# Reordering the stages ahead of the experts of a decoder-layer step

## The reference, cut to what matters

```python
h = x + W_o( sigmoid(g_a) * Mamba2_SSD(n) + sigmoid(g_b) * ShortConv(n) ),  n = RMSNorm(x)
h = h + CrossAttn(RMSNorm(h), mem)    # 4 heads over 256 memory tokens
h = h + MoE(RMSNorm(h))               # top-4 of 32 experts, clamped SwiGLU, softmax router
y = RMSNorm(h)

def rmsnorm(x, g):
    y = xf * lax.rsqrt(jnp.mean(xf * xf, axis=-1, keepdims=True) + EPS)
    return (y * g.astype(jnp.float32)).astype(x.dtype)

# samples, one step of the recurrence (per head h, p: 64 rows, n: 128 columns)
s = jnp.exp(dtt * a)[:, :, None, None] * s + jnp.einsum('bh,bhp,bhn->bhpn', dtt, xt, bt)
y = jnp.einsum('bhpn,bhn->bhp', s, ct)

# short convolution and merge
u, new_sbuf = causal_dwconv(sconv_buf, sc_c * sc_v, lw['w_sconv'], None)
merged = jax.nn.sigmoid(g_a) * y_a + jax.nn.sigmoid(g_b) * (sc_b * u)
```

## Time and profile before

| what | value |
| --- | --- |
| median of 3 runs | 1551.15 us (1549.5 to 1552.83) |
| profiled execution: own time / span in the trace | 1553.77 / 1551.6 us |
| PE busy | 1462.9 us, 94% |
| DVE / ACT / POOL busy | 449.6 / 216.3 / 26.1 us |
| mean granted TensorE clock | 0.968 |
| HBM traffic | 490.31 MB, mean 316 GB/s |

### The profile page before, as it was taken

How to read it: one execution, slowest core, us unless ns; L and a number is a source line. 1 busy time by engine, 2 the same in 40 slices (tenths; PEclk the granted TensorE clock), 3 DMA queues, 4 the chain that set the end, 5 groups by cost and what they waited for, 6 DMA issues and landing times.

```text
span 1551.6 us, 16659 instructions
## 1 busy us (share of the span) xinstructions
PE 1462.9 (94%) x6505; PEld 745.5 (48%) x6505; DVE 449.6 (29%) x891; ACT 216.3 (14%) x392; POOL 26.1 (2%) x42
## 2 busy tenths in 40 slices
PE   7999999988598799999999999999999999999997
PEld 5888888665377583333333333333333333333332
DVE  2630030486613423222222222212213213213213
ACT  2111311311112221101101101001001001001002
POOL 0000000012000000000000000000000000000000
PEclk8999999989699888999999999999999999999999
DMA  5634443337124683999999999999999999999993
GB/s 156 248 131 145 162 161 121 115 118 248 68 109 152 253 356 120 399 430 429 427 429 427 429 429 428 428 428 428 429 429 427 429 428 428 430 427 429 429 428 152
DMA packets 68776, 490.31 MB, mean 316 GB/s; under 512 B 8483, under 2 KB 9915, under 8 KB 44157
## 3 DMA queue, kind: packets, MB, share of 16 engines
q1 hardware_dynamic: 65372, 478.61, 75.0%
q0 software_dynamic: 3184, 11.31, 2.2%
q10 hardware_dynamic: 196, 0.07, 0.0%
HBM read 481.94 MB, written 8.19 MB: 316 GB/s over the span
## 4 chain that ended last, share of the span: by engine, by line
PE 70%; DMA 21%; DVE 6%; issue 2%; SPq 1%; ACT 1%; DVEq 0%; ACTq 0%
PE bank L1124 65%; DMA ring<-in_w_gate_up 18%; PE bank L1133 4%; DMA projT<-in_state_ssm 2%; DVE projT L942 2%; DMA out<-projT 1%; SPq L386 0%; DVE conv L901 0%; DVE projT L831 0%; DVE projT L879 0%; DVE projT L883 0%; DVE projT L881 0%; DMA flat<-in_x_sample 0%; DVE xnT L704 0%; DVE projT L854 0%
## 5 line engine op out<-in xcount | busy, mean ns | idle before, releaser
L1124 PE MATMUL bank<-ring,projT 128*64 128x512 f32 (+1 forms) x2112 | 461.2, 596 | 20.4 <-DMA ring<-in_w_gate_up 19.9
L1124 PEld LDWEIGHTS bank<-ring,projT 128*64 128x64 f32 (+1 forms) x2112 | 149.7, 136 | 315.4 <-issue 312.8
L1124 PE MATMUL bank<-xnT,ring 128*128 128x264 f32 x1152 | 258.5, 388 | 3.1 <-DVE xnT L704 3.1
L1124 PEld LDWEIGHTS bank<-xnT,ring 128*128 128x128 f32 x1152 | 219.8, 191 | 41.4 <-issue 3.5
L1124 PE MATMUL bank<-flat,projT 128*64 128x512 f32 (+1 forms) x552 | 236.6, 582 | 0.0
L1124 PE MATMUL bank<-conv,projT 128*64 128x512 f32 x512 | 225.8, 594 | 0.0
L1124 PE MATMUL bank<-projT 128*128 128x512 f32 (+1 forms) x472 | 210.0, 584 | 8.3 <-DVE flat L846 2.4
L457 ACT ACTIVATE projT<-bank 128x512 f32<-128x512 f32 (+3 forms) x189 | 93.7, 515 | 559.5 <-PE bank L1124 556.5
L1124 PEld LDWEIGHTS bank<-flat,projT 128*64 128x64 f32 (+1 forms) x552 | 77.6, 143 | 139.4 <-issue 137.6
L1124 PEld LDWEIGHTS bank<-projT 128*128 128x128 f32 (+1 forms) x472 | 63.5, 169 | 152.6 <-issue 103.5
L1085 DVE TENSOR_SCALAR projT<-bank 128x512 f32<-128x512 f32 x32 | 20.6, 686 | 343.9 <-PE bank L1124 343.9
(11 more groups left out here) (234 smaller groups left out, 814.4 us busy)
## 6 DMA issues: line engine op xcount, KB each, us to landing
ring<-in_w_gate_up SPq DMA_DIRECT2D x96, 2048.0 KB, 16.2
ring<-in_w_down SPq DMA_DIRECT2D x32, 2048.0 KB, 13.1
ring<-in_w_in SPq DMA_DIRECT2D x16, 2048.0 KB, 11.0
flat<-in_w_gate_up SPq DMA_DIRECT2D x16, 2048.0 KB, 14.0
conv<-in_w_gate_up SPq DMA_DIRECT2D x16, 2048.0 KB, 18.4
flat<-in_w_down SPq DMA_DIRECT2D x16, 2048.0 KB, 15.8
conv<-in_w_down SPq DMA_DIRECT2D x16, 2048.0 KB, 20.2
ring<-in_cache_mem_k SPq DMA_DIRECT2D x4, 2048.0 KB, 7.7
```

The lines of the kernel that those rows point to most:

```text
L1124: last[0] = pe.matmul(out, lhsT, rhs, start=start, stop=stop)
```

## The change

The kernel computes the same outputs from the same inputs. What differs, in the order of execution:

- **Norms.** The mean squares of x and of the memory are taken from the token-major tiles as they arrive: one fused multiply-and-sum on DVE per tile (`mean_squares`, three for x, two for the memory), a root on ACT, a reciprocal of a few columns. A matmul of the reciprocal column (broadcast) against the identity spreads it into a bank (`rbc`, `mbc`), from which DVE scales. dt is projected feature-major in eight matmuls of 264 columns and turned by four transposes (`dtt`).
- **Projections.** xBC first (`xb`), with dt, the memory's transposes and norm, and the small transposes between its blocks; then `cc` and `cv` (DVE multiplies out of the bank), with the kept rows' transposes and those of xs and B between; then `cb` and `z`, with the ten scan steps after chosen blocks (`STEP_AT`); then `ga` with the key blocks, and `gb` with the group norm's matmuls. The loops over blocks are unrolled.
- **Samples' states.** Their B and C rows are transposed once (`brow`, eight transposes), written to a scratch tensor in HBM by POOL, and read back by POOL for each sample with the row broadcast to 128 partitions, into two buffers. The state has four buffers instead of two; the first loads are issued during the scan. POOL waits for `state_read` of a sample, then issues the row load two samples on, the state's write, and, after the landing of the write before, the state load three samples on.
- **Query.** ACT scales h by the gain alone into `xnT` (no norm), DVE adds the squares of the eight blocks in `rinv`, one ones-matmul sums over partitions (`h1ss`, behind the second `q` block), and DVE applies root, reciprocal and 1/16 to the q blocks as it empties their banks.
- **Attention.** `att`, `qb`, `pT`, `o` and the last two value blocks are placed between `q` blocks and among each other; `qb` goes by halves of the heads. Six slots are used instead of four for the chunks, the last two (`flat`, `conv`) from the cached keys on.
- **SP.** The small loads are spread between the first five chunks (`early`). The first experts' loads wait for other jobs.

The loop over experts, `xo`, the router and all after them are untouched.

```diff
...
-PLAN += [("dec", 1, D_)]
-FILL = {1: "vp", 2: "kp", 4: "kp", 5: "kp", 6: "kp"}
-for _n in range(TS):
-    PLAN += [("bcs", 2, D_)]
-    if _n in FILL:
-        PLAN += [(FILL[_n], 1, A_)]
-PLAN += [("kT", 4, A_), ("gn", 4, A_), ("wo", 8, D_), ("h1ss", 1, A_), ("q", 8, A_), ("att", 4, A_),
-         ("qb", 8, D_), ("pT", 4, A_), ("qb", 8, D_), ("o", 2, A_), ("sT", 1, D_), ("o", 2, A_), ("sP", 1, A_),
-         ("so", 4, A_), ("sx", 4, A_), ("xo", 8, D_), ("rt", 1, D_), ("xtok", 6, A_), ("rank", 1, D_)]
...
+STEP_AT = {("cb", 2): 0, ("cb", 3): 1, ("cb", 5): 2, ("cb", 7): 3, ("z", 0): 4, ("z", 2): 5, ("z", 3): 6,
+           ("z", 5): 7, ("z", 6): 8, ("z", 7): 9}
+for _j in range(8):
+    PLAN += [("cb", 1, D_)]
+    if _j < 2:
+        PLAN += [("sin", 1, A_), ("srow", 1, A_)]
+    PLAN += ssd_step(STEP_AT["cb", _j]) if ("cb", _j) in STEP_AT else []
+for _j in range(8):
+    PLAN += [("z", 1, A_)]
+    PLAN += ssd_step(STEP_AT["z", _j]) if ("z", _j) in STEP_AT else []
+PLAN += [("fin", 2, A_), ("dec", 1, D_), ("brow", 2, A_)]
+for _j in range(4):
+    PLAN += [("ga", 2, A_), ("kp", 1, A_)]
+for _j in range(8):
+    PLAN += [("gb", 1, A_)]
+    if _j >= 4:
+        PLAN += [("gn", 1, A_)]
+PLAN += [("kT", 4, A_), ("vp", 2, A_), ("wo", 8, D_), ("q", 2, D_), ("h1ss", 1, A_), ("q", 3, D_), ("att", 1, A_),
+         ("qb", 2, D_), ("q", 1, D_), ("att", 1, A_), ("qb", 2, D_), ("q", 1, D_), ("qb", 2, D_), ("q", 1, D_),
+         ("qb", 2, D_), ("pT", 2, A_), ("att", 2, A_), ("qb", 2, D_), ("o", 1, A_), ("qb", 2, D_), ("vp", 1, A_),
+         ("qb", 2, D_), ("o", 1, A_), ("qb", 2, D_), ("vp", 1, A_), ("sT", 1, D_), ("pT", 2, A_), ("o", 2, A_),
+         ("sP", 1, A_), ("so", 2, A_), ("sx", 1, A_), ("so", 1, A_), ("sx", 1, A_), ("so", 1, A_), ("sx", 2, A_),
+         ("xo", 8, D_), ("rt", 1, D_), ("xtok", 6, A_), ("rank", 1, D_)]
+
...
+            ("cc0", w_in(4112), 0, ("filled", "xb", 3)), ("cv0", w_in(5136), 1, ("filled", "xb", 7)),
...
+            ("K0", cache("cache_mem_k", 0), 4, ("flat_free",)), ("K1", cache("cache_mem_k", 1), 5, ("conv_free",)),
...
+            for i, (name, src, where, free) in enumerate(WEIGHTS):
+                early(i)
...
+            for j, name, k in ((2, "so", 1), (4, "so", 1), (5, "so", 3), (0, "so", 3), (1, "xo", 3), (3, "xo", 7)):
...
+            def rows_load(b):
+                pool.dma_start(bcr[b % 2].rearrange("p j g n -> p (j g n)"),
+                               rows_hbm[b].partition_broadcast(P)).then_inc(bcr_in[b % 2], 16)
...
+            emptied(pool, "brow", 1)
+            pool.dma_start(rows_hbm[:, :], brow).then_inc(S["rows_kept"], 16)
+            pool.wait_ge(S["rows_kept"], 16)
+            rows_load(0)
+            rows_load(1)
+            for b in range(TS):
+                pool.wait_ge(S["state_read"], b + 1)
+                if b + 2 < TS:
+                    rows_load(b + 2)
+                pool.dma_start(sout[b], sst[b % 4]).then_inc(state_out[b % 4], 16)
+                if b >= 1 and b + 3 < TS:
+                    pool.wait_ge(state_out[(b - 1) % 4], 16)
+                    state_load(b + 3)
...
+            for k in range(KB):
+                emptied(s, "wo", k)
+                copy(xnT[:, k, :], hT[:, k, :], pcol(NXA + k)).then_inc(S["xn_ready"], 1)
+                s.activation(sqh[:, k, :], hT[:, k, :], ACT.Square).then_inc(S["h_squared"], 1)
...
+            def mean_squares(src, junk_, col, n, sem_):
+
+                v.tensor_tensor_reduce(junk_, src, src, 1.0, 0.0, ALU.mult, ALU.add, rtok[0:n, col:col + 1]).then_inc(sem_, 1)
...
+            def scale_rows(job, dst, src, n, gain, out):
+
+                b = filled(v, job)
                 for k in range(KB):
-                    v.scalar_tensor_tensor(out=dst[:, k, 0:n], in0=src[:, k, 0:n], scalar=pcol(gain + k), in1=r,
-                                           op0=ALU.mult, op1=ALU.mult).then_inc(S[out], 1)
-
-            emptied(v, "par0")
...
-                b = filled(v, "bcs", 2 * i)
-                done(v.tensor_tensor(out=by_group(prod), in0=rows_of(b), in1=by_group(bc(dtx[:, :, i], P)), op=ALU.mult))
-                emptied(v, "bcs", 2 * i)
+                v.wait_ge(bcr_in[i % 2], 16 * (i // 2 + 1))
+                rows = [bcr[i % 2][:, j].unsqueeze(2).to_broadcast([P, G, 2, P]) for j in range(2)]
+                st(v.tensor_tensor(out=by_group(prod), in0=rows[0], in1=by_group(bc(dtx[:, :, i], P)), op=ALU.mult))
...
+            for k in range(KB):
+                emptied(v, "gb", k)
+                st(v.tensor_tensor(out=gbs[:, k, :], in0=gbs[:, k, :], in1=u[:, k, :], op=ALU.mult))
+                if k == 0:
+                    v.wait_ge(S["a_ready"], KB)
+                v.tensor_tensor(out=merged[:, k, :], in0=yT[:, k, :], in1=gbs[:, k, :], op=ALU.add)\
+                    .then_inc(S["merged_ready"], 1)
...
+            def add_square(k, sq, count):
+
+                v.wait_ge(S["h_squared"], count + k + 1)
+                return v.tensor_tensor(out=rinv[:], in0=rinv[:] if k > 1 else sq[:, 0, :], in1=sq[:, k, :], op=ALU.add)
...
+            def scale_q(k):
+
+                b = filled(v, "q", k)
+                done(v.scalar_tensor_tensor(out=qT[:, k, :], in0=b[:, 0:T], scalar=1.0 / 16, in1=rinv[:],
+                                            op0=ALU.mult, op1=ALU.mult), "q", k)
...
-            sum_squares("xss", sqx, T, "x_squared", lambda k: k + 1)
...
+            b = free_bank(pe, "rbc")
+            pe.wait_ge(S["x_rms"], 2)
+            for t, (c, n) in enumerate(TILES):
+                mm(b[:, c:c + n], rtok[0:n, t:t + 1].to_broadcast([n, P]), ident[0:n, 0:n])
+            close("rbc")
...
+            b = free_bank(pe, "dt")
+            for k in range(KB):
+                mm(b[0:H, 0:T], wdt[:, k, :], xnT[:, k, :], k == 0, k == KB - 1)
+            close("dt")
...
+            for k in range(8):
+                project("cb", (k,), "cb", xnT)
+                if k < 2:
+                    chunk_start(k)
+                    cv_rows(k)
+                if ("cb", k) in STEP_AT:
+                    ssd_step(STEP_AT["cb", k])
+            for k in range(8):
...
+                b = free_bank(pe, "brow", j)
+                for i in range(G):
+                    turn(b[0:TS, i * P:i * P + P], conv[:, 8 + 4 * j + i, TP:T])
...
+            for k in range(4):
+                project("ga", (2 * k, 2 * k + 1), "ga", xnT)
+                project_kv("kp", k)
+            for k in range(8):
+                project("gb", (k,), "gb", xnT)
+                if k >= 4:
+                    g = k - 4
+                    b = free_bank(pe, "gn", g)
+                    for i in range(2):
+                        pe.wait_ge(S["u_squared"], 2 * g + i + 1)
+                        mm(b[:, 0:T], ones[:], sqg[:, 2 * g + i, :], i == 0, i == 1)
...
+            b = free_bank(pe, "h1ss")
+            pe.wait_ge(S["h1_summed"], 1)
+            mm(b[:, 0:T], ones[:], rinv[:])
...
```

More of the change, by code:

```diff
@@ new lines, in _, with cc @@
+            xb(3, 4)
+            mem_cols(0, 2)
+            xb(4, 5)
+            mem_cols(2, 4)
+            xb(5, 6)
+            move("par1", 0, par[:, 1, 0:24], 24)
+            s.wait_ge(S["mem_summed"], 2)
+            root(rtok, slice(4, 6), P, S["mem_root"])
+            xb(6, 9)
+            move("mst", 0, msT[:], 384)
+            xb(9, 10)
+            move("sst", 0, ssT[:], 128)
+            xb(10, 16)
+            def cc(k):
+                move("cc", k, projT[:, SCC + k, :], T)
@@ new lines, in _ @@
+            s.wait_ge(S["fin_out"], 16)
+            for k in range(4):
+                move("kT", k, kT[:, 2 * k:2 * k + 2, :], 512)
+            for k in range(2):
+                copy_kv("vp", k)
+            s.activation(small[:, 300:301], eps[:], ACT.Sqrt)
+            for k in range(KB):
+                emptied(s, "wo", k)
+                copy(xnT[:, k, :], hT[:, k, :], pcol(NXA + k)).then_inc(S["xn_ready"], 1)
+                s.activation(sqh[:, k, :], hT[:, k, :], ACT.Square).then_inc(S["h_squared"], 1)
@@ new lines, in _ @@
+            dtk, dta = dtm[:, 0:2], dtm[:, 2:4]
+            emptied(v, "par1")
+            scale_rows("mbc", mnT, mnT, NM, NMEM, "mem_normed")
+            for k in range(7, 12):
+                convolve(k)
+            b = filled(v, "acum")
+            done(v.tensor_copy(small[:, 0:64], b[:, 0:64]), "acum")
+            emptied(v, "acum")
+            st(v.tensor_tensor(out=small[:, 64:80], in0=small[:, 32:48], in1=small[:, 0:16], op=ALU.subtract))
+            st(v.tensor_tensor(out=small[:, 80:96], in0=small[:, 64:80], in1=small[:, 48:64], op=ALU.add))
@@ L759, in _ @@
+            v.tensor_tensor(out=small[:, 96:112], in0=small[:, 48:64], in1=small[:, 16:32],
+                            op=ALU.subtract).then_inc(S["acum_read"], 1)
+            for k in range(12, XB):
+                convolve(k)
             emptied(v, "mst")
@@ new lines, in probabilities, with sample_scores @@
+            def probabilities(hh):
```

(39 more changed lines are left out.)

1354 lines of the change are left out of this document (730 added, 624 removed).

## The result

The changed kernel takes 1456.24 us (median of 4 runs, 1452.88 to 1457.5) against 1551.99 for the kernel before. One of the four runs behind that 1551.99 was slow (1718.09 us) and is left out of the ratio; the other three took 1549.5 to 1552.83. The ratio is 0.9385, with a 95% interval of 0.9361 to 0.9408. The profiled execution took 1457.5 us and has a span of 1455.3. The forecast was 1464, from 1455 to 1476: the time lies in it, 1.2 us above its low end.

A forecast was written before the change was run, and what follows sets the result against it. PE, in order, bounds most work ahead of the unchanged DMA-heavy expert loop, so gains there arrive whole. Work 33.0, waits 43.7 and clock 15 make 91.7, less 5 for hand-overs: 87 us, 1464; forecast 1455 to 1476, full range 1455 to 1496.

The forecast's parts named there:

- (a): Start: first projection block begins near 16.6 us instead of 40.55, with PE waiting 2 us of that.
- (b): Scan: each step has one or two projection blocks behind it, so PE's 4.9 us idle goes to 0.
- (c): Samples' states: about 10 us until the first sample; DVE side needs 66 us beside 73.8 of PE, cover 8.
- (d): Group norm: 3.7 us per group against 4.45 of PE; kT and two value blocks hide the merge.
- (e): Query from h scaled by gain only: last block ready about 1.2 us after wo, covered by 3.1 of matmuls.
- (f): Attention: PE's 65 us is longer than DVE's work; about 4.5 us idle stays, samples' softmax and step to xo.
- the first one of the sum: PE work that goes ahead of the loop: norm sums, dt product, B and C spread, query norm; 33.0 us.
- The clock's own term: Five stages from 269.24 to 541.24: a PE that never rests gains 6.5 to 29.5 us, taken as 15.
- The first (interleaving doesn't fill the gaps): Rival: waits in scan and attention also hold the projections behind them; about 17 us come back, 1481; chance 0.13.
- The second, in which DVE and POOL shut each other out: Rival: three POOL issues per sample add to DVE's chain in the states' stage; 13 us late, 1477; chance 0.04.
- The third rival: Samples' row loads land late, at 20.6 us; 38 us late, 30 behind the cover, 1494; chance 0.09.
- The fourth and fifth: Rivals: row landings at 45 us make it slower, 1567, chance 0.02; DMA-bound loop lets nothing arrive, 1551, chance 0.01.

The follow-up runs named there:

- two-pass run: Changed kernel with the last reduction of each sample on DVE made three times, two more passes per sample: 1473.11 us.
- one more pass per sample: Changed kernel with the last reduction of each of the eight samples on DVE made twice: 1457.22 us.
- run with later loads: Changed kernel with each sample's B and C row load issued one sample later: 1479.93 us.
- five parts undone: Changed kernel with scan in one piece, rows spread by PE, first norm by ones, query from normalised h, attention in one piece: 1501.88 us.
- run with ga moved: Changed kernel with the eight ga blocks ahead of the samples' stage instead of beside it: 1475.99 us.

## Why the prediction was right, and where not

**The bound.** Right: the loop's length stood to 0.03 us, and the loop started as much earlier as the work ahead of it ended. It started 9 us ahead of the 512 I had given: 3.9 more of idle time went than I had summed, the 5 taken off for hand-overs were not needed, and the stretch from `xo` on was 1.3 shorter, less 0.6 that work and clock together fell short.

**Idle time.** (a) The first block was put at 16.6 and came at 16.73; of PE's last wait ahead of it 0.86 us are the first chunk's, landed 14.55 after its issue at 2.14. (b) The scan's 4.9 went, and 5.8 us of idle time came back when the order was undone. (c) The time to the first rows was put at 10: DVE waited 11.1 for them. The chain ended (gate by z) at 298.0, 68.3 after the start of the stage, where 63.5 of my sum stood, so 5 late. The cover for added work was 8, as said, but by luck: 2.6 of it were left at PE's end, and 4.4 more lay in DVE's waits for rows, which the sum didn't have. By my own sign I should have been wrong here, since DVE waited 14.8 us in all for rows where I had allowed 8; the sign didn't fit the sum, which has 10 us until the first sample, and PE felt none of it. (d) The group norm's four turns followed PE at 4.45 each, without a wait. (e) No wait at q. (f) 1.5 us stayed in attention instead of 4.5. Idle time left is 9.5 where I had 13.4, and nothing of the 5 us was needed that I took off for hand-overs.

**Work and clock: two terms mis-sized, with opposite signs.** I said 33.0 of work and 15 of clock, and it was 23.0 and 24.4. The sum, 48.0 for 47.4, hid it. The step that failed is the first one of the sum: the dt product (7.5) and the memory's sum (5.9) were priced by rows 5 that lie between 27.1 and 40.5, and up to 39.0 the clock was at its lower level. 6.0 us (half of 12) of these durations are clock and not work. I counted them as work, and then said that at the start the clock brings no gain: one gain under the wrong name. The other 4.0 are prices. The sum over x took 4.9 when it was put back, not 6.3, and I set the added matmuls at nought, where the two broadcasts take 1.7 and 0.6 and the turns of dt 0.4. The rows that were priced by rows at full clock came out: the spread of B and C at 13.7 was 14.1.

The clock's own term was about the five stages from 269.24 on, and there the windows give 18.4 us lost (1.3, 4.0, 4.4, 3.9 and 4.8) where I took 15. That is 37 us at the lower level, well inside my bounds of 13 and 59. I took a point near the low end because clock and rest go together. In the trace the clock fell during waits or within a us behind them, and the lower level reached well into the work that followed. The two-pass run shows it in small: 6 us of work behind the wait. So 4.0 too much of work met 3.4 too little of clock, and that the two nearly cancel is luck.

**Clock at the start.** I expected the lower level up to about 29. The granted clock of the profile's rows reads 1.00 from the start to 475 us. Still, the first matmuls are slow: 32 records in 9.69 us, and 7.39 later. About 2.3 us are lost there, not 6. Why they are slow while the clock reads 1.00 is open.

**From `xo` to the loop.** Taken at 57.7, it was 56.4. The runs give 53.2 to 58.2 for the same instructions, and two of them, at 58.2, lie beyond the 57.7 that I had set as a sign. In one (the changed kernel) the transposes run at the lower clock and take 5.3 and the twelve gather matmuls 10.5. In another (one more pass per sample) 7.4 for the gather:

```profile
480.52 5.31 PE L1353 MATMUL bank<-ident,hT 128*128 128x128 f32 x24
...
489.83 10.53 PE L1342 MATMUL bank<-projT 128*128 128x512 f32 x12 [2.15 <-DVE small L1241]
```

```profile
491.23 7.44 PE L1343 MATMUL bank<-projT 128*128 128x512 f32 x12 [2.15 <-DVE small L1242]
```

When in this stretch the clock falls differs from run to run, by 2 to 3 us of time.

**The rivals.** The first (interleaving doesn't fill the gaps) would have shown waits for m and for probabilities; from the first block to `xo` no wait of PE is longer than 0.6 us. With the order undone in both places `xo` starts 6.9 and 16.0 later, 23 us together, so what it put at stake, about 17, was there. The second, in which DVE and POOL shut each other out, would have stretched passes or issues. A sample with two issues of POOL inside it (DVE, then POOL):

```profile
245.80 1.22 DVE L1064 TENSOR_REDUCE projT<-projT 128x8 f32<-128x1024 f32 x1
...
246.58 0.91 POOL L518 DMA_DIRECT2D out<-projT  x1
247.06 1.23 DVE L1056 TENSOR_TENSOR projT<-projT 128x1024 f32<-128x1024 f32 x1
```

The issue of 0.91 us lies across two passes of 1.22 and 1.23, and neither grew. The Trainium skill (SBUF — State Buffer, SBUF: two separate sides) says that a DMA issued from POOL's queue waits for its descriptors while DVE runs a two-port performance mode. The trace shows neither of the two held up by the other; it doesn't tell whether these passes run in such a mode, so it is no test of the page's rule. The third rival happened in part, 3.7 us in the chain, and the run with later loads shows what late rows cost, 26 us there. It was given 30 behind the cover at a landing of 20.6, which no row load came near (4.5 to 11.4 us in the changed kernel). The fourth and fifth didn't happen.

**What is not settled.** With the five parts undone `xo` starts at 495.3, 45.9 ahead of the kernel before: 24.7 of idle time, 14.8 of clock and 6.5 of work. The samples' stage (the two states in flight, the place of the projections) and the order of the first norms are what is left to explain it. The run with ga moved shows 23 us for one of its pieces. The others were not measured one by one, so about half of these 45.9 us is put down to them without a run.

## What to carry to other kernels

Price an operation by a row only after looking at the granted clock of that row's own stretch, and at a row of the same shape elsewhere; and count what a full-rate engine wins once, in one term: work at full rate, idle time and clock are three columns, and each can be read from short windows. Where an in-order engine is the bound, look for work that waits for nothing (projections here) and keep it back for the chain on the other engines that is the longest; where it stands was worth more (23 us) than any operation removed (14 us). And slack is found not only where the bounding engine arrives, but also inside the chain that it waits for: add work there and see.

## What the runs showed of the hardware that I had not expected

The granted clock of the rows and the durations can part: early in the execution the clock reads 1.00 and 32 records of 128x264 take 9.69 us, 9.23 in the second trace of the same kernel, and 7.39 from 30 us on. The Trainium skill (TensorE: Matmul & The Clock Gate, Seeing it yourself) warns that the trace's clock events can be unreliable; this agrees with it.

A wait of PE was dearer than its length, but not always: with the busy time lost to the clock behind it, 1.95 us of standing cost 1.95, 12.2 cost 15.3 and 20.8 cost 22.8, all at the same place. The length of one wait doesn't settle it, since in the scan in one piece no wait was longer than 1.8 us, and 1.6 us were lost behind them. And the landing of a load of one row to 128 partitions moved between 6.3 and 8.8 us (medians) from one order of issue to another. The same half MB as a state took 4.4 in the kernel before and 7.3 to 8.4 in the changed one, so the form of the load alone doesn't explain it.
